# Six norms of a two-model forward pass in float32: token tiles, row halves, and who makes the low halves of x

## The chip, the core and the metric

One core of a Trainium2 chip. The metric is the device time of one execution in microseconds (us): the median of the runs.

## The reference

Two blocks of a sequence model run one behind the other on x of 256 tokens by 1024 channels. The first block is a gated convolution and a three-pattern dilated attention, merged; the second has two layers, each an attention (12 heads over the tokens, 4 over 256 memory tokens) and a convolutional feed-forward part (FFN, 2 x 2816 wide). Between the parts stand norms over the channels, two rms norms (y = x · rsqrt(mean(x²) + eps) · g) and four layer norms:

```python
def layer_norm(x, g, b):
    xf = x.astype(jnp.float32)
    mu = xf.mean(-1, keepdims=True)
    var = jnp.square(xf - mu).mean(-1, keepdims=True)
    return ((xf - mu) * lax.rsqrt(var + LN_EPS) * g + b).astype(x.dtype)
...
        x = layer_norm(ALPHA * x + mix, ln1_g[layer], ln1_b[layer])
        ffn = conv_ffn(x, ffn_w_in[layer], ffn_conv_w[layer], ffn_conv_b[layer], ffn_w_out[layer])
        x = layer_norm(ALPHA * x + ffn, ln2_g[layer], ln2_b[layer])
```

## The kernel before

**Split products.** Every large matmul is float32 made of three: each operand is a high half (rounded to the matmul type) and a low half (the rest), and high·high, high·low and low·high are summed in PSUM. The weights come from HBM as one stream of blocks of 128 x 1024 through a ring of three buffers. For each block SyncE loads `raw`, ScalarE copies it to the high half `wh` (L417), VectorE subtracts to the low half `wl` (L815), and TensorE uses both. A block's load waits until the low half of the block three before it is made (`split_l`); its high half waits until TensorE has used that block (`used`).

**Order of work.** Each engine has a list of instructions written out by hand, with semaphores between them. `refill(i, b)` stands in ScalarE's and in VectorE's list and makes the half of block b + 3.

**The row blocks.** The output product of a part (`row`, L1378 to L1380) adds one block to `ysum`, four PSUM banks: two token tiles of 128 (t) by two column halves (n), 12 matmuls of 512 columns. In the last block the first token tile signals `half`, the second `used`.

**A norm.** Six of them, n0 to n5; n0 and n1 are rms norms, the others layer norms. By token tile: VectorE adds the residual to `ysum` and sums (L861), ScalarE squares with a running sum (L431), GpSimd makes 1/sqrt (L297, L299), VectorE scales z (L889, or L893 without mean; L934 in n0). TensorE transposes z in eight 128 x 128 pieces a tile into four PSUM banks (`turn_x`, L1398), between which it multiplies memory keys or values, which don't need x. Then x is made, transposed, channel tile by channel tile (k = 0 to 7): VectorE multiplies by gain and adds shift into `xf` (L833, L836; ScalarE for k = 6, 7, L450), ScalarE makes the high half `xh` (L442), and the low half `xl` = xf - xh is made by VectorE for even k (L825) and by GpSimd for odd k (L322). TensorE takes all three products of one k before the next (`two_stationary`, L1342 to L1344, 48 matmuls of 256 columns; in n3 the value blocks at L1759; in n0 `row`). Behind its low halves GpSimd makes the next residual, x in token layout: z times gain, and plus shift in n2 to n4, two or four instructions of 128 x 1024 (`tail`, L312 and L315).

**Around n2 and n4** an FFN follows: TensorE opens the `ysum` banks with zero matmuls (L1483), ScalarE and VectorE make the first product of the FFN (L712, L1239, L1242, L718, L1250, L722, L825), and the loop goes on with `stationary` (L1330 to L1332, 24 matmuls of 256 columns) and `row`.

```python
            def tail(nm, shift):
                pool.wait_ge(gb_in, 16 + 32 * (norms.index(nm) - 1))
                for t in range(NT):
                    norm_wait(pool, nm, "z", t + 1)
                    last = pool.tensor_tensor(x_tok[:, t, :], z[:, t, :], gb[:, 0, :], ALU.mult)
                    if shift:
                        chain.link(last)
                        last = pool.tensor_tensor(x_tok[:, t, :], x_tok[:, t, :], gb[:, 1, :], ALU.add)
                    last.then_inc(S[nm, "x"], 1)
```

## Time and profile before

| what | us |
|---|---|
| median of 3 runs | 1001.85 (1001.05 to 1003.83) |
| the profiled execution | 1001.48 |
| its span, first to last instruction | 999.7 |
| TensorE busy | 948.9 |
| VectorE busy | 664.5 |
| ScalarE busy | 527.0 |
| GpSimd busy | 127.9 |

The span is the profiled part of one execution, 1.8 us shorter than its own time. In the trace's rows PE is TensorE, DVE VectorE, ACT ScalarE, POOL GpSimd. The start and the length of an instruction are given; where two rows of one engine overlap, the second starts while the first drains, so the distance of two starts is the cost of one in a row of many. The length of a row holds time in which the instruction stood started but could not go on.

### The profile page before, as it was taken

To read this page: it belongs to the slowest core of one execution; us is meant where nothing else is said; L and a number is where in the kernel's file an instruction comes from. 1 tells how busy PE (TensorE), PEld (TensorE's weight loads), DVE (VectorE), ACT (ScalarE), POOL (GpSimd) and SP (SyncE) were. 2 spreads that over 40 slices of the span, in tenths; PEclk is the share of its full clock that TensorE was granted. 3 is DMA by queue.
4 is the path that set the end of the run, shared out by engine and by line. 5 is a ranking of instruction groups with operands and counts; after the bars stand their busy time and mean duration, and the time that the engine had idled before them with its cause. 6 is when DMAs were issued, how large, how long until landed. Compare 5 with 4: busy or idle time off the path is not lost.

```text
span 999.7 us, 19995 instructions
## 1 busy us (share of the span) xinstructions
PE 948.9 (95%) x7006; PEld 859.3 (86%) x7006; DVE 664.5 (66%) x1212; ACT 527.0 (53%) x967; POOL 127.9 (13%) x154
## 2 busy tenths in 40 slices
PE   8999999999999888999799999998899989999995
PEld 5899999999899877757699999987788679999995
DVE  5566666666666857965866666678567666666666
ACT  5545555555444648754555555545565455555553
POOL 3000000000100402630600000006100150000001
PEclk9999999999999999999999999999999999999998
DMA  7555555556465375314265555553754346555552
GB/s 256 181 190 178 178 178 182 178 175 226 148 210 188 125 254 158 120 37 148 86 231 190 187 188 189 189 193 108 243 179 152 105 148 205 188 184 189 184 189 77
DMA packets 48226, 172.89 MB, mean 173 GB/s; under 512 B 6031, under 2 KB 6479, under 8 KB 48060
## 3 DMA queue, kind: packets, MB, share of 16 engines
q1 hardware_dynamic: 44732, 159.78, 47.9%
q0 software_dynamic: 3456, 12.61, 4.1%
q8 instruction: 24, 0.39, 0.2%
q14 instruction: 14, 0.11, 0.0%
HBM read 171.29 MB, written 1.07 MB: 172 GB/s over the span
## 4 chain that ended last, share of the span: by engine, by line
PE 77%; DVE 10%; ACT 6%; DMA 4%; issue 2%; POOL 1%; SPq 0%; POOLq 0%; ACTq 0%; DVEq 0%
PE bank L1330 17%; PE bank L1331 17%; PE bank L1332 17%; PE ysum L1378 6%; PE ysum L1380 6%; PE ysum L1379 6%; DVE sb_wl L815 5%; DMA sb_raw<-in_stream 4%; ACT sb_wh L417 2%; PE bank L1409 1%; PE ysum L1416 1%; PE ysum L1423 1%; ACT sb_xh L442 1%; DVE sb_z L861 1%; ACT sb_pr L462 1%
## 5 line engine op out<-in xcount | busy, mean ns | idle before, releaser
L815 DVE TENSOR_TENSOR sb_wl<-sb_raw,sb_wh 128x1024 fp32r<-128x1024 f32 x300 | 388.4, 1297 | 169.2 <-ACT sb_wh L417 168.3
L1330 PE MATMUL bank<-sb_xh,sb_wh 128*128 128x256 f32 x1360 | 383.3, 282 | 3.2 <-DVE sb_t_a L1242 2.5
L1331 PE MATMUL bank<-sb_xl,sb_wh 128*128 128x256 f32 x1360 | 379.8, 279 | 0.0
L1332 PE MATMUL bank<-sb_xh,sb_wl 128*128 128x256 f32 x1360 | 379.8, 279 | 0.0
L417 ACT ACTIVATE sb_wh<-sb_raw 128x1024 fp32r<-128x1024 f32 x300 | 315.0, 1055 | 116.2 <-PE ysum L1380 46.7
L1330 PEld LDWEIGHTS bank<-sb_xh,sb_wh 128*128 128x128 f32 x1360 | 256.3, 188 | 12.6 <-DVE sb_t_a L1242 3.5
L1332 PEld LDWEIGHTS bank<-sb_xh,sb_wl 128*128 128x128 f32 x1360 | 257.9, 190 | 0.0
L1331 PEld LDWEIGHTS bank<-sb_xl,sb_wh 128*128 128x128 f32 x1360 | 255.4, 188 | 1.5
L1378 PE MATMUL ysum<-sb_wh,sb_mh 128*128 128x512 f32 x208 | 81.7, 393 | 3.6 <-DVE sb_ml L825 3.6
L1379 PE MATMUL ysum<-sb_wl,sb_mh 128*128 128x512 f32 x208 | 81.7, 393 | 0.0
L1380 PE MATMUL ysum<-sb_wh,sb_ml 128*128 128x512 f32 x208 | 81.6, 393 | 0.0
L297 POOL TENSOR_SCALAR sb_st<-sb_st 128x1 f32<-128x1 f32 x12 | 4.3, 358 | 492.6 <-ACT sb_pr L431 488.5
L722 ACT ACTIVATE sb_mh<-sb_t_c 128x256 fp32r<-128x256 f32 x44 | 18.4, 419 | 90.4 <-DVE sb_t_c L1250 90.4
L712 ACT ACTIVATE sb_t_a<-bank,sb_convf 128x256 f32<-128x256 f32 x44 | 24.9, 566 | 47.3 <-PE bank L1332 43.0
L1378 PEld LDWEIGHTS ysum<-sb_wh,sb_mh 128*128 128x128 f32 x208 | 39.5, 190 | 10.4 <-issue 3.9
L462 ACT ACTIVATE sb_pr<-sb_sc,sb_mx 128x128 f32<-128x128 f32 x80 | 35.6, 448 | 23.1 <-DVE sb_mx L909 23.1
L1380 PEld LDWEIGHTS ysum<-sb_wh,sb_ml 128*128 128x128 f32 x208 | 39.5, 190 | 8.3
L1379 PEld LDWEIGHTS ysum<-sb_wl,sb_mh 128*128 128x128 f32 x208 | 39.3, 189 | 6.4
L1239 DVE SCALAR_TENSOR_TENSOR sb_t_a<-bank,sb_convf,sb_t_a 128x255 f32<-128x255 f32 x44 | 21.2, 482 | 27.0 <-ACT sb_t_a L712 26.9
L1330 PE MATMUL bank<-sb_mixh,sb_wh 128*128 128x256 f32 x128 | 36.3, 283 | 0.8 <-DVE sb_wl L815 0.8
L825 DVE TENSOR_TENSOR sb_ml<-sb_t_c,sb_mh 128x256 fp32r<-128x256 f32 x44 | 21.2, 481 | 23.9 <-ACT sb_mh L722 23.9
L1331 PE MATMUL bank<-sb_mixl,sb_wh 128*128 128x256 f32 x128 | 36.0, 281 | 0.0
(265 smaller groups left out, 1439.0 us busy)
## 6 DMA issues: line engine op xcount, KB each, us to landing
sb_raw<-in_stream SPq DMA_DIRECT2D x300, 512.0 KB, 3.3
sb_bias<-rel_rows POOLq DMA_DIRECT2D x12, 384.0 KB, 3.8
sb_bias<-in_alibi POOLq DMA_DIRECT2D x8, 256.0 KB, 3.1
sb_gb<-in_ln_g POOLq DMA_DIRECT2D x4, 512.0 KB, 4.1
sb_gb<-in_ln_b POOLq DMA_DIRECT2D x4, 512.0 KB, 6.5
sb_x_tok<-in_x SPq DMA_DIRECT2D x2, 512.0 KB, 3.9
sb_memf<-in_mem_t POOLq DMA_DIRECT2D x1, 1024.0 KB, 6.2
out<-sb_x_tok SPq DMA_DIRECT2D x2, 512.0 KB, 2.6
```

Of the source, the lines that this page charges most:

```text
L417: act.activation(wh[slot][:, :, :], raw[slot][:, :, :], ACT.Copy).then_inc(split_h, 1)
L462: act.activation(to[:, branch, h, cols], src, ACT.Exp, bias=mx[:, c:c + 1], scale=-1.0, accum_out=den[:, c:c + 1]).then_inc(S[ph, "exp"], 1)
L712: act.activation(t_a[:, :], bank[0][:, 0:T], ACT.Identity, bias=convf[:, layer, bass.ds(i, 1), 3], scale=convf[:, layer, bass.ds(i, 1), 2] ...
L815: dve.tensor_tensor(wl[slot][:, :, :], raw[slot][:, :, :], wh[slot][:, :, :].bitcast(F32), ALU.subtract).then_inc(split_l, 1)
L825: dve.tensor_tensor(dst, src, high, ALU.subtract).then_inc(s, 1)
L1239: cf.link(dve.scalar_tensor_tensor(out=t_a[:, 1:T], in0=bank[0][:, 0:T - 1], scalar=convf[:, layer, bass.ds(i, 1), 1], in1=t_a[:, 1:T], op ...
L1330: pe.matmul(out, wh[slot][:, k, :], mov_h(k), start=k == 0, stop=False)
L1331: pe.matmul(out, wh[slot][:, k, :], mov_l(k), start=False, stop=False)
L1332: last = pe.matmul(out, wl[slot][:, k, :], mov_h(k), start=False, stop=k == KT - 1)
L1378: pe.matmul(out, th[:, t * P:(t + 1) * P], hw, start=start, stop=False)
L1379: pe.matmul(out, th[:, t * P:(t + 1) * P], lw, start=False, stop=False)
L1380: last = pe.matmul(out, tl[:, t * P:(t + 1) * P], hw, start=False, stop=stop)
```

## The change

1. **The last two row blocks by token tile** (`last_rows`): tile 0 of both blocks, then tile 1 of both. `half` comes after 12 of the 24 matmuls and not after 18; the second block's operand is needed after 6 and not after 12. VectorE's low half for one later block, which stood ahead of the sums, stands behind them (`soon`).
2. **Rows of z in halves**: VectorE scales 512 columns at a time and TensorE transposes each half when it is there.
3. **High halves from PSUM**: ScalarE makes all eight `xh` straight from the transposed z, with gain and shift, not from `xf`. VectorE still fetches k = 0 to 5 into `xf`, ScalarE 6 and 7, behind the high halves. VectorE fetches a bank only when ScalarE is through with it (k = 4, 5 the other way round, except in n0 and n3).
4. **Low halves**: VectorE makes seven (all but k = 1), GpSimd k = 1 alone. GpSimd's `tail` stands right behind that one.
5. **Low x last**: `two_stationary` takes the products with `xh` of all eight k, then those with `xl`; the value blocks of n3 and the row blocks of n0 do the same inside one block (`x_rows`). The memory products between the transposes are cut in other places (`memory_keys`; in n3 the first value block of the memory needs no norm and stands ahead of the transposes, in bank 3).
6. In n4 ScalarE makes the high half of block `B_FFN1 + 2` ahead of x.

```diff
+FETCHED = {nm: (0, 1, 2, 3, 4, 5) if nm in ("n0", "n3") else (4, 5, 0, 1, 2, 3)
+           for nm in ("n0", "n1", "n2", "n3", "n4")}
+LOW_DVE, LOW_POOL = (0, 2, 3, 4, 5, 6, 7), (1,)
...
             def low_odd(nm):
-                for k in range(1, KT, 2):
+                for k in LOW_POOL:
+                    norm_wait(pool, nm, "xf", FETCHED[nm].index(k) + 1)
             def norm_high(nm, g, b):
-                def high(k):
-                    if k < 6:
-                        norm_wait(act, nm, "xf", k + 1)
-                    else:
-                        norm_wait(act, nm, "xf_act", k - 5)
-                    act.activation(xh[:, k, :], xf[:, k, :], ACT.Copy).then_inc(S[nm, "xh"], 1)
-                for k in range(4):
-                    high(k)
-                norm_wait(act, nm, "turned", KT)
+                shift = [0.0 if b is None else gbt[:, b, k:k + 1] for k in range(KT)]
+                for k in range(KT):
+                    norm_wait(act, nm, "turned", k // 2 * 2 + 2)
+                    if k in (4, 5) and nm not in ("n0", "n3"):
+                        norm_wait(act, nm, "xf", 2)
+                    act.activation(xh[:, k, :], turned_x(nm, k), ACT.Identity, scale=gbt[:, g, k:k + 1],
+                                   bias=shift[k]).then_inc(S[nm, "xh"], 1)
                 for k in (6, 7):
-                    if k == 7:
-                        high(4)
-                    act.activation(xf[:, k, :], turned_x(nm, k), ACT.Identity,
-                                   scale=gbt[:, g, k:k + 1], bias=0.0 if b is None else gbt[:, b, k:k + 1]
-                                   ).then_inc(S[nm, "xf_act"], 1)
-                for k in range(5, KT):
-                    high(k)
+                    act.activation(xf[:, k, :], turned_x(nm, k), ACT.Identity, scale=gbt[:, g, k:k + 1],
+                                   bias=shift[k]).then_inc(S[nm, "xf_act"], 1)
             def exps(ph, branch, h, causal=True, to=pr):
...
                 def fetch(k):
-                    norm_wait(dve, nm, "turned", k // 2 * 2 + 2)
+                    if nm in ("n0", "n3") or k < 4:
+                        norm_wait(dve, nm, "xh", k // 2 * 2 + 2)
+                    else:
+                        norm_wait(dve, nm, "turned", k // 2 * 2 + 2)
...
-                def low_even(k):
+                def low_of(k):
+                    if k < 6:
+                        norm_wait(dve, nm, "xf", FETCHED[nm].index(k) + 1)
+                    else:
+                        norm_wait(dve, nm, "xf_act", k - 5)
...
-                for k in range(0, 6, 2):
-                    fetch(k)
-                    fetch(k + 1)
-                    low_even(k)
-                    if k == 0 and between is not None:
-                        between()
-                low_even(6)
+                if nm in ("n0", "n3"):
+                    for k in FETCHED[nm]:
+                        fetch(k)
+                        if k in LOW_DVE:
+                            low_of(k)
+                        if k == 0 and between is not None:
+                            between()
+                else:
+                    for k in FETCHED[nm][:4]:
+                        fetch(k)
+                    low_of(0)
+                    for k in FETCHED[nm][4:]:
+                        fetch(k)
+                    for k in LOW_DVE[1:5]:
+                        low_of(k)
+                for k in (6, 7):
+                    low_of(k)
+            def norm_sum(nm, last_block, alpha, centred, x_from, fill=(), soon=None):
...
+                if soon is not None:
+                    refill(0, soon)
...
-                    if centred:
-                        norm_wait(dve, nm, "mean", t + 1)
-                        dve.tensor_scalar(z[:, t, :], z[:, t, :], st[:, 4 + t:5 + t],
-                                          st[:, 10 + t:11 + t], ALU.add, ALU.mult).then_inc(S[nm, "z"], 1)
-                    else:
-                        norm_wait(dve, nm, "sum", t + 1)
-                        dve.tensor_scalar(z[:, t, :], z[:, t, :], st[:, 10 + t:11 + t], None,
-                                          ALU.mult).then_inc(S[nm, "z"], 1)
+                    norm_wait(dve, nm, "mean" if centred else "sum", t + 1)
+                    for n in range(2):
+                        part = z[:, t, n * 512:(n + 1) * 512]
+                        if centred:
+                            dve.tensor_scalar(part, part, st[:, 4 + t:5 + t], st[:, 10 + t:11 + t],
+                                              ALU.add, ALU.mult).then_inc(S[nm, "z"], 1)
+                        else:
+                            dve.tensor_scalar(part, part, st[:, 10 + t:11 + t], None,
+                                              ALU.mult).then_inc(S[nm, "z"], 1)
...
+                if k1 == KT:
+                    last.then_inc(used, 1)
             def two_stationary(b, nm):
                 ready(b + 2)
+                for k in range(KT):
+                    norm_wait(pe, nm, "xh", k + 1)
+                    for n in range(2):
+                        out, s = bank[n][:, 0:T], slot_of(b + n)
+                        pe.matmul(out, wh[s][:, k, :], xh[:, k, :], start=k == 0, stop=False)
+                        pe.matmul(out, wl[s][:, k, :], xh[:, k, :], start=False, stop=False)
                 for k in range(KT):
                     x_ready(nm)(k)
                     for n in range(2):
-                        out, s = bank[n][:, 0:T], slot_of(b + n)
-                        pe.matmul(out, wh[s][:, k, :], xh[:, k, :], start=k == 0, stop=False)
-                        pe.matmul(out, wh[s][:, k, :], xl[:, k, :], start=False, stop=False)
-                        last = pe.matmul(out, wl[s][:, k, :], xh[:, k, :], start=False, stop=k == KT - 1)
+                        last = pe.matmul(bank[n][:, 0:T], wh[slot_of(b + n)][:, k, :], xl[:, k, :],
+                                         start=False, stop=k == KT - 1)
                         if k == KT - 1:
                             last.then_inc(used, 1)
-            def wide(slot, part, bk, sh, sl):
...
-                    norm_wait(pe, nm, "xl_pool" if k % 2 else "xl_dve", k // 2 + 1)
+                    norm_wait(pe, nm, "xh", k + 1)
+                    if k in LOW_POOL:
+                        norm_wait(pe, nm, "xl_pool", LOW_POOL.index(k) + 1)
+                    else:
+                        norm_wait(pe, nm, "xl_dve", LOW_DVE.index(k) + 1)
                 return wait
...
+                    last.then_inc(used, 1)
+            def x_rows(nm, slot, parts, out, n_first=False):
+                def part(w, j, n):
+                    j = n if n_first else j
+                    return w[slot][:, 4 * j:4 * j + 4, :].rearrange("p k c -> p (k c)")
+                for k, j, t, n in parts:
+                    norm_wait(pe, nm, "xh", k + 1)
+                    tok = slice(t * P, (t + 1) * P)
+                    pe.matmul(out(t, n)[:, :], xh[:, k, tok], part(wh, j, n), start=k == 0, stop=False)
+                    pe.matmul(out(t, n)[:, :], xh[:, k, tok], part(wl, j, n), start=False, stop=False)
+                for k, j, t, n in parts:
+                    x_ready(nm)(k)
+                    last = pe.matmul(out(t, n)[:, :], xl[:, k, t * P:(t + 1) * P], part(wh, j, n),
+                                     start=False, stop=k == KT - 1)
                 last.then_inc(used, 1)
...
+            def last_rows(b, first, second, half, second_made=()):
+                ready(b + 1)
+                row_tile(slot_of(b), *first, 0, False, False)
+                ready(b + 2)
+                for made in second_made:
+                    pe.wait_ge(*made)
+                row_tile(slot_of(b + 1), *second, 0, False, True).then_inc(half, 1)
+                row_tile(slot_of(b), *first, 1, False, False).then_inc(used, 1)
+                row_tile(slot_of(b + 1), *second, 1, False, True).then_inc(used, 1)
...
                 ready(k + 1)
-                x_ready("n0")(k)
-                row(slot_of(k), xh[:, k, :], xl[:, k, :], k == 0, k == KT - 1)
+                x_rows("n0", slot_of(k), [(k, 0, t, n) for t in range(NT) for n in range(2)],
+                       lambda t, n: bank[4 + 2 * t + n], n_first=True)
...
             def memory_keys(b, nm):
-                for n in range(2):
+                def keys(n, k0=0, k1=KT):
                     ready(b + n + 1)
-                    stationary(slot_of(b + n), bank[2 + n][:, 0:T], lambda k: memh[:, k, :], lambda k: meml[:, k, :])
-                    turn_x(nm, n)
+                    stationary(slot_of(b + n), bank[2 + n][:, 0:T], lambda k: memh[:, k, :], lambda k: meml[:, k, :],
+                               k0, k1)
+                keys(0)
+                turn_x(nm, 0)
+                keys(1, 0, KT // 2)
+                turn_x(nm, 1)
+                keys(1, KT // 2, KT)
...
             ffn("f0", B_FFN0, "n2")
+            ready(B_VM + 1)
+            wide(slot_of(B_VM), 0, bank[3], memh, meml)
+            ready(B_VM + 2)
             norm_wait(pe, "n3", "mean", 1)
-            for n in range(2):
-                ready(B_VM + n + 1)
-                wide(slot_of(B_VM + n), n, bank[4], memh, meml)
-                turn_x("n3", n)
+            for t in range(NT):
+                turn_x("n3", t)
+                wide(slot_of(B_VM + 1), 1, bank[3], memh, meml, (t,))
```

The places in the order of instructions. VectorE at n2, from the sum of token tile 1 to the first low half of the FFN's product. Before (`sb_xl<-sb_pt,sb_xh` is a low half of x, `sb_pt<-ysum` a fetch into xf, `sb_wl` a weight block's low half):

```order
L861 SCALAR_TENSOR_TENSOR sb_z,sb_st<-sb_x_tok,ysum1 128x1024 [waits used]
L866 TENSOR_SCALAR sb_st<-sb_st 128x1 [waits dve_chain]
L889 TENSOR_SCALAR sb_z<-sb_z,sb_st 128x1024 [waits norm_mean,norm_rstd] x2
...
L836 TENSOR_SCALAR sb_pt<-ysum0,sb_gbt 128x256 [waits norm_turned] x2
L825 TENSOR_TENSOR sb_xl<-sb_pt,sb_xh 128x256 [waits norm_xh]
L836 TENSOR_SCALAR sb_pt<-ysum0,sb_gbt 128x256 [waits norm_turned] x2
L825 TENSOR_TENSOR sb_xl<-sb_pt,sb_xh 128x256 [waits norm_xh]
L836 TENSOR_SCALAR sb_pt<-ysum1,sb_gbt 128x256 [waits norm_turned] x2
L825 TENSOR_TENSOR sb_xl<-sb_pt,sb_xh 128x256 [waits norm_xh] x2
L815 TENSOR_TENSOR sb_wl2<-sb_raw2,sb_wh2 128x1024 [waits split_h]
```

and now:

```order
L881 TENSOR_SCALAR sb_st<-sb_st 128x1 [waits dve_chain]
L813 TENSOR_TENSOR sb_wl2<-sb_raw2,sb_wh2 128x1024 [waits split_h]
L908 TENSOR_SCALAR sb_z<-sb_z,sb_st 128x512 [waits norm_mean,norm_rstd]
...
L837 TENSOR_SCALAR sb_pt<-ysum1,sb_gbt 128x256 [waits norm_turned] x2
L837 TENSOR_SCALAR sb_pt<-ysum0,sb_gbt 128x256 [waits norm_xh] x2
L823 TENSOR_TENSOR sb_xl<-sb_pt,sb_xh 128x256 [waits norm_xh,norm_xf]
L837 TENSOR_SCALAR sb_pt<-ysum0,sb_gbt 128x256 [waits norm_xh] x2
L823 TENSOR_TENSOR sb_xl<-sb_pt,sb_xh 128x256 [waits norm_xh,norm_xf] x4
L823 TENSOR_TENSOR sb_xl<-sb_pt,sb_xh 128x256 [waits norm_xh,norm_xf_act] x2
L813 TENSOR_TENSOR sb_wl2<-sb_raw2,sb_wh2 128x1024 [waits split_h]
```

The low halves of x went from four to seven, six of them in one row behind the last fetch, and a weight block's low half moved between the sums and z. GpSimd at the same place, before:

```order
L322 TENSOR_TENSOR sb_xl<-sb_pt,sb_xh 128x256 [waits norm_xh] x4
L312 TENSOR_TENSOR sb_x_tok<-sb_z,sb_gb 128x1024 [waits norm_z,gb_in]
L315 TENSOR_TENSOR sb_x_tok<-sb_x_tok,sb_gb 128x1024 [waits pool_chain]
L312 TENSOR_TENSOR sb_x_tok<-sb_z,sb_gb 128x1024 [waits norm_z]
L315 TENSOR_TENSOR sb_x_tok<-sb_x_tok,sb_gb 128x1024 [waits pool_chain]
```

and now:

```order
L328 TENSOR_TENSOR sb_xl<-sb_pt,sb_xh 128x256 [waits norm_xh,norm_xf]
L317 TENSOR_TENSOR sb_x_tok<-sb_z,sb_gb 128x1024 [waits norm_z,gb_in]
L320 TENSOR_TENSOR sb_x_tok<-sb_x_tok,sb_gb 128x1024 [waits pool_chain]
L317 TENSOR_TENSOR sb_x_tok<-sb_z,sb_gb 128x1024 [waits norm_z]
L320 TENSOR_TENSOR sb_x_tok<-sb_x_tok,sb_gb 128x1024 [waits pool_chain]
```

The four instructions of the tail (two in n1) stand three low halves nearer to the start of x. TensorE's 48 matmuls of x in n2 began, for each k, with this, before:

```order
L1342 MATMUL bank0<-sb_xh,sb_wh0 128x256 [waits norm_xl_dve,split_l]
L1343 MATMUL bank0<-sb_xl,sb_wh0 128x256
L1344 MATMUL bank0<-sb_xh,sb_wl0 128x256
L1342 MATMUL bank1<-sb_xh,sb_wh1 128x256
L1343 MATMUL bank1<-sb_xl,sb_wh1 128x256
L1344 MATMUL bank1<-sb_xh,sb_wl1 128x256
```

and now begin with four matmuls for each k that wait for the high half alone:

```order
L1361 MATMUL bank0<-sb_xh,sb_wh0 128x256 [waits norm_xh,split_l]
L1362 MATMUL bank0<-sb_xh,sb_wl0 128x256
L1361 MATMUL bank1<-sb_xh,sb_wh1 128x256
L1362 MATMUL bank1<-sb_xh,sb_wl1 128x256
L1361 MATMUL bank0<-sb_xh,sb_wh0 128x256 [waits norm_xh]
```

The 16 matmuls with `xl` follow behind all of these.

## Rows read from the trace of the kernel before

**Rows 1.** The page, part 1: busy us (share of the span) and instructions.
```profile
PE 948.9 (95%) x7006; PEld 859.3 (86%) x7006; DVE 664.5 (66%) x1212; ACT 527.0 (53%) x967; POOL 127.9 (13%) x154
```

**Rows 2.** What TensorE waited for, whole span: total us, times, longest us.
```profile
PE ysum L1378 <- DVE sb_ml L825: 3.6, 2, 2.0
PE bank L1330 <- DVE sb_t_a L1242: 2.5, 2, 2.0
```

**Rows 3.** Timeline, norm n2: start us, us, engine, instruction, count, idle before and releaser.
```profile
467.67 0.42 DVE L825 TENSOR_TENSOR sb_mixl<-bank,sb_mixh 128x256 fp32r<-128x256 f32 x1
469.21 0.39 PE L1378 MATMUL ysum<-sb_wh,sb_mixh 128*128 128x512 f32 x1
471.95 0.28 PE L1330 MATMUL bank<-sb_memh,sb_wh 128*128 128x256 f32 x1
475.30 0.81 DVE L889 TENSOR_SCALAR sb_z<-sb_z,sb_st 128x1024 f32<-128x1024 f32 x1 [0.92 <-POOL sb_st L299]
476.18 1.09 PE L1398 MATMUL ysum<-sb_ident,sb_z 128*128 128x128 f32 x8 [1.31 <-DVE sb_z L889]
477.57 2.35 DVE L815 TENSOR_TENSOR sb_wl<-sb_raw,sb_wh 128x1024 fp32r<-128x1024 f32 x2
481.38 0.42 DVE L825 TENSOR_TENSOR sb_xl<-sb_pt,sb_xh 128x256 fp32r<-128x256 f32 x1
481.95 0.36 PE L1342 MATMUL bank<-sb_xh,sb_wh 128*128 128x256 f32 x1 [0.98 <-DVE sb_xl L825]
483.08 0.55 ACT L450 ACTIVATE sb_pt<-ysum,sb_gbt 128x256 f32<-128x256 f32 x1
483.10 0.99 DVE L836 TENSOR_SCALAR sb_pt<-ysum,sb_gbt 128x256 f32<-128x256 f32 x2
487.88 1.04 PE L1483 MATMUL ysum<-sb_zeros 128*128 128x512 bf16 x4
```

**Rows 4.** Timeline, just behind n2: GpSimd and VectorE, and what TensorE waited for.
```profile
486.52 2.39 POOL L312 TENSOR_TENSOR sb_x_tok<-sb_z,sb_gb 128x1024 f32<-128x1024 f32 x1
486.99 2.99 DVE L815 TENSOR_TENSOR sb_wl<-sb_raw,sb_wh 128x1024 fp32r<-128x1024 f32 x1 [1.03 <-ACT sb_wh L417]
488.98 3.23 POOL L315 TENSOR_TENSOR sb_x_tok<-sb_x_tok,sb_gb 128x1024 f32<-128x1024 f32 x1
...
490.95 0.38 PE L1330 MATMUL bank<-sb_xh,sb_wh 128*128 128x256 f32 x1 [2.03 <-DVE sb_t_a L1242]
492.17 3.34 POOL L312 TENSOR_TENSOR sb_x_tok<-sb_z,sb_gb 128x1024 f32<-128x1024 f32 x1
494.11 1.68 DVE L825 TENSOR_TENSOR sb_ml<-sb_t_c,sb_mh 128x256 fp32r<-128x256 f32 x1 [0.49 <-ACT sb_mh L722]
495.59 2.43 POOL L315 TENSOR_TENSOR sb_x_tok<-sb_x_tok,sb_gb 128x1024 f32<-128x1024 f32 x1
495.94 0.52 PE L1378 MATMUL ysum<-sb_wh,sb_mh 128*128 128x512 f32 x1 [2.00 <-DVE sb_ml L825]
```

**Rows 5.** Timeline, VectorE and TensorE behind norm n3.
```profile
688.40 14.19 DVE L815 TENSOR_TENSOR sb_wl<-sb_raw,sb_wh 128x1024 fp32r<-128x1024 f32 x5 [0.98 <-ACT sb_wh L417]
691.50 0.50 PE L1759 MATMUL ysum<-sb_wh,sb_xh 128*128 128x512 f32 x1 [2.32 <-DVE sb_wl L815]
```

**Rows 6.** Busy time by engine, granted clock (PEclk) of two stretches, at n2 and n4.
```profile
496.40:499.40 3.00, 3.00 (x9) 2.32 (x8) 3.00 (x2) 0.00 (x0) 2.70 (x3) 0.50 0.00 0
796.70:803.30 6.60, 6.06 (x29) 5.69 (x28) 5.35 (x11) 4.87 (x11) 3.62 (x5) 0.50 0.01 2
```

**Rows 7.** Timeline: last product before n1; TensorE behind n1, behind n4, in n0.
```profile
323.27 0.43 DVE L1042 SCALAR_TENSOR_TENSOR sb_ml<-sb_t_c,sb_mh 128x256 fp32r<-128x256 f32 x1 [0.54 <-ACT sb_mh L541]
344.64 0.35 PE L1358 MATMUL bank<-sb_wh,sb_xh 128*128 128x256 f32 x1 [2.06 <-DVE sb_wl L815]
806.18 1.04 PE L1483 MATMUL ysum<-sb_zeros 128*128 128x512 bf16 x4
18.40 0.50 PE L1378 MATMUL ysum<-sb_wh,sb_xh 128*128 128x512 f32 x1 [0.94 <-DVE sb_wl L815]
```

More of the change, by code:

```diff
@@ L1326, in _, with stationary @@
         def _(pe):
-            def stationary(slot, out, mov_h, mov_l):
-                for k in range(KT):
+            def stationary(slot, out, mov_h, mov_l, k0=0, k1=KT):
+                for k in range(k0, k1):
                     pe.matmul(out, wh[slot][:, k, :], mov_h(k), start=k == 0, stop=False)
@@ L1365, in wait @@
                 def wait(k):
-                    norm_wait(pe, nm, "xl_pool" if k % 2 else "xl_dve", k // 2 + 1)
-                return wait
-            def row(slot, th, tl, start, stop, half=None, bank7_read=None):
-                for t in range(NT):
-                    for n in range(2):
-                        out = bank[4 + 2 * t + n][:, :]
-                        if bank7_read is not None and t == n == 1:
-                            pe.wait_ge(*bank7_read)
-                        hw = wh[slot][:, 4 * n:4 * n + 4, :].rearrange("p k c -> p (k c)")
-                        lw = wl[slot][:, 4 * n:4 * n + 4, :].rearrange("p k c -> p (k c)")
-                        pe.matmul(out, th[:, t * P:(t + 1) * P], hw, start=start, stop=False)
-                        pe.matmul(out, th[:, t * P:(t + 1) * P], lw, start=False, stop=False)
-                        last = pe.matmul(out, tl[:, t * P:(t + 1) * P], hw, start=False, stop=stop)
-                    if t == 0 and half is not None:
-                        last.then_inc(half, 1)
-                last.then_inc(used, 1)
+                    norm_wait(pe, nm, "xh", k + 1)
@@ new lines, in wait, with row_tile @@
+                    if k in LOW_POOL:
+                        norm_wait(pe, nm, "xl_pool", LOW_POOL.index(k) + 1)
+                    else:
+                        norm_wait(pe, nm, "xl_dve", LOW_DVE.index(k) + 1)
+                return wait
+            def row_tile(slot, th, tl, t, start, stop, bank7_read=None):
+                for n in range(2):
+                    out = bank[4 + 2 * t + n][:, :]
+                    if bank7_read is not None and t == n == 1:
+                        pe.wait_ge(*bank7_read)
+                    hw = wh[slot][:, 4 * n:4 * n + 4, :].rearrange("p k c -> p (k c)")
+                    lw = wl[slot][:, 4 * n:4 * n + 4, :].rearrange("p k c -> p (k c)")
+                    pe.matmul(out, th[:, t * P:(t + 1) * P], hw, start=start, stop=False)
+                    pe.matmul(out, th[:, t * P:(t + 1) * P], lw, start=False, stop=False)
+                    last = pe.matmul(out, tl[:, t * P:(t + 1) * P], hw, start=False, stop=stop)
+                return last
@@ L1706, in finish @@
                 memory_out(ph, 1)
-                rows(6)
-                pe.wait_ge(S[ph, "ol"], 2)
-                rows(7)
+                last_rows(r0 + 6, (oh[:, 6, :], ol[:, 6, :]), (oh[:, 7, :], ol[:, 7, :]), half, ((S[ph, "ol"], 2),))
             pe.wait_ge(S["p3", "fill"], 3)
@@ L1751, in _ @@
                 ready(b + 1)
[L1752 to L1762 removed]
+                x_rows("n3", slot_of(b), [(2 * n + j, j, t, 0) for j in range(2) for t in range(NT)],
+                       lambda t, n: bank[5 + t])
             for n in range(2):
```

77 lines of the change are left out of this document (31 added, 46 removed).

## The prediction

> **What bounds the kernel now.** The page's busy line comes first: TensorE works 948.9 of 999.7 us [rows 1]. So a change can win only in the 51 us in which TensorE stands, and lose only where it makes TensorE stand. The table of TensorE's waits says for whom: in the FFNs behind n2 and n4 it waits for the low half of the product (3.6 us in two waits) and for the convolution's last tap (2.5 us in two) [rows 2]. The timeline of n2 shows the norm's chain [rows 3]: the last row block starts at 469.21, the memory keys at 471.95 (12 matmuls of 512 columns in 2.74 us, 0.228 each), z is scaled from 475.30 for 0.81 us, the first transposes start at 476.18 after 1.31 us of standing, the first x matmul at 481.95 after 0.98, and the 48 x matmuls are through at 487.88, where the bank opening starts: 0.12 us each. They hardly wait: x, at 1.4 us for two channel tiles on VectorE, keeps up.
>
> The rows behind n2 show the thing I build on [rows 4]. GpSimd's tail has four instructions of 1024 columns. Its first starts at 486.52 and ends at 488.91, which is 2.39 us. VectorE's weight subtraction starts at 486.99 and needs 2.99 us, though two of the same took 2.35 together at 477.57 [rows 3]: it ends 1.07 us after GpSimd's instruction, so it stood until then. GpSimd's second begins at 488.98, takes 3.23 us and so waited for VectorE. A subtraction of 256 columns, 0.42 us elsewhere [rows 3], takes 1.68 us at 494.11 and ends at 495.79, 0.28 us after GpSimd's third (492.17 + 3.34 = 495.51). Behind n3 five weight subtractions take 14.19 us [rows 5]; at 1.17 each they would take 5.9. So a VectorE subtraction with both inputs in SBUF and a GpSimd instruction exclude each other, and with both queues full they take turns, one each. A turn of GpSimd costs 2.2 us (2.39 and 2.43 undisturbed, less the start). Fetches from PSUM are not stopped.
>
> The Trainium skill has a narrower rule in "Advanced Engine Details and Errata", VectorE Performance Modes: the port is shared, and GpSimd and the two-port modes of VectorE block each other. A subtraction of two tensors isn't in such a mode; by that rule none of the low halves would wait; what the time would be then stands with rival (e). The same skill's "SBUF — State Buffer", Who interferes with whom, counts an instruction with two SBUF inputs in as well, and the 1.68 us side with it.
>
> **The change, part by part.** Times are dates of the profiled execution (1001.48 us; the median of the three runs is 0.37 above it).
>
> *Last two row blocks.* The second block's low half is now wanted after 6 matmuls. At n2 it is there at 467.67 + 0.42 = 468.09 [rows 3], the 6 matmuls end at 469.21 - 1.37 = 467.84: TensorE stands 0.3 us. At n1 the operand ends at 323.70 [rows 7] and 6 matmuls earlier than needed before means 323.01: 0.75 us. I take 0.25 in n3, 0.3 in n4. In return tile 0's chain starts 2 us earlier; but a weight subtraction of 1.2 us stands between the sums and z, and tile 1's sum starts 0.3 later, so z starts at 475.3 as before. Only its first half, 0.42 instead of 0.81, brings the transposes from 476.18 to 475.8. Two more VectorE instructions a tile cost nothing there, since TensorE transposes the first half meanwhile. SyncE's load behind the moved weight subtraction starts 3 us later; its block is used in the FFN's loop, 20 us on, which covers it.
>
> *x at n2, with nobody in the way.* From 475.8: 16 transposes (1.8) and the 24 key matmuls (2.9) end at 480.5. ScalarE's high halves from PSUM cost 0.45 each (0.55 a row, less overlap) [rows 3], the first at 478.6, so the 32 matmuls with xh run without a gap to 484.3. VectorE: z until 477.5, two weight blocks to 479.8, six fetches of 0.46 and one low half to 482.9, six low halves of 0.34 to 485.0. The 16 matmuls with xl then end at 486.2, against 487.88: **1.7 us won.**
>
> *x at n2 with the tail.* GpSimd has one low half and starts its tail at 482.5, before VectorE's six low halves, where it stood 4 us later before. The first turn lasts to 484.7; then a low half (0.3), a turn (2.2), and so on: low halves 2, 3, 4 and 5 end at 485.0, 487.5, 490.0 and 492.5, numbers 6 and 7 at 493.2. The x matmuls end at 493.7: **5.8 us late.** In exchange GpSimd is through when the FFN starts. The waits of 2.03 and 2.00 us at 490.95 and 495.94 [rows 4] shrink to 0.5 and 0.5 (the chain itself is 0.56 + 2 x 0.48 us against 1.04 of bank opening): 3.0 back. n2 costs **+2.8**.
>
> *The others, same working.* n4: here nothing but zero matmuls stands between rows and transposes, so z's first half decides, at 793.9; x could start at 796.2 and, unblocked, be through at 801.9. VectorE's low halves 2 to 7 are due from 799.3, the tail starts at 799.0, and four turns put the last at 810.0: the x matmuls, at 806.18 through [rows 7], end at 810.4, +4.2; its waits of 1.6 and 0.5 [rows 2] (less n2's share) and 0.65 for weights behind give back 1.6: **+2.6**. n3: the first value block of the memory no longer waits for the sum (its 1.0 us goes, and x comes that much earlier), low halves alternate with fetches, and four turns fall between them as well; the third value block's weights, ready for 691.50 [rows 5], come behind the seventh low half at 694.1, at 695.3: +3.8, less 1.7, since the weight blocks then come faster than TensorE's 2.74: **+2.1**. n1 has two turns and starts 0.8 late (the 0.75 above): x ends at 344.2, the next weights at 345.0 against 344.64 [rows 7]: **+0.4**. n0 has no tail: its first matmul comes 1.2 us earlier, but VectorE reaches the third weight block 0.2 later than for 18.40 [rows 7], and TensorE waits for that: **+0.2**. n5: tile 0 earlier, tile 1, which ends the kernel, the same: 0 (between -0.4 and +0.3).
>
> *The clock.* Behind waits of 2 us in n2 and in n4 the granted clock was 0.50, that is 1.2 and not 2.4 GHz, for 3.0 and 6.6 us at least [rows 6]; a stretch of 3.4 us at it costs 1.7. No row shows what a stall of 6 to 8 us brings. Bounds: nothing new (n2 and n4 had theirs) and one more stretch in each of three norms, 5.1. I take 2.0, a stretch more in n3 and a little in n4, since their stalls are the long ones.
>
> Sum: 0.2 + 0.4 + 2.8 + 2.1 + 2.6 + 0 + 2.0 = **+10.1**: 1011.6 for the profiled execution, 1012.0 for the median.
>
> **Rivals.** (a) *VectorE's row of low halves keeps the port.* In n1, n2 and n4 six short ones stand in a row; if GpSimd's first gets in only where VectorE pauses, the gains stay. For it: none of my rows has two 256-column subtractions in a row beside the tail. Against it: behind n3 five subtractions stood in a row and GpSimd had its turn in between. n1 then gives -1.5 (the next weights meet the tail, at 343.1 for 344.64), n2 -1.7, n4 -4.3 (x done at 801.9: the highs run at full clock), n3 +2.1 as above, n0 +0.2: -5.2, so 996.7. It decides if the tail's start slips from 482.5 to beyond 485.0. (b) *Half hidden:* the first turn falls into the matmuls with xh, which TensorE has until 484.3, in n2, n3 and n4, and the clock doesn't fall: 10.1 less 3 x 2.2 and less 2.0 is +1.5: 1003. It decides if low half 2 comes before the turn and not behind it. (c) *The clock goes down and stays* in all four norms: 5 to 7 instead of 2, 1017. (d) *The change doesn't do what it says:* the early half buys nothing since z starts when it did; that is in my sum already, and a z at 474.3, where 1/sqrt would allow it, would shift everything by 1 us a norm: 1008. (e) *No blocking of subtractions at all.* Then the gains and the waits behind both fall in: n1 -3.3, n2 -1.7 - 3.0, n3 -3.4 - 1.7, n4 -4.3 - 1.6, n0 +0.2: 983. The 1.68 us for 0.42 [rows 4] speak against it, and nothing for it. It is what the skill's narrower rule would give.
>
> **How the numbers follow.** Forecast with its spread, (c) and (d): 0.76, of which (c) 0.08 and (d) 0.08. Rival (a) 0.13, (e) 0.01, (b) 0.10. The measurement can tell about 0.3%, 3 us, from no change. Faster is (a) and (e), 0.14, with 0.01 from (b)'s lower side, 0.15; the same is (b), 0.1; slower is the rest, 0.75. The range reaches from (b)'s lower side, 1001, to one clock stretch above (c), 1019; (a) and the tails are left out, 0.2 in all. The forecast's own range is 1006 to 1018.
>
> **What would show it.** Right: low halves 2 to 5 (now L823) at 0.42 to 2.5 us long in n1 to n4, mean near 1.2; TensorE's waits for `sb_xl` of 2 us and more, several a norm, 20 us in all and more; the waits for the tap and for `sb_ml` under 1 us each; the clock at 0.50 behind n3. The first transposes of n2 some 0.4 us earlier relative to the last row block. Wrong: low halves at 0.42 us throughout with the tail behind them (rival a), or x matmuls through earlier than before.

## The result and the profile after

| | before | changed |
|---|---|---|
| median, lowest, highest, us (5 runs each) | 1001.85, 1001.05, 1003.83 | 1010.25, 1009.00, 1014.62 |
| ratio to before | | 1.0087, 95% interval 1.0071 to 1.0103 |
| profiled execution, span, us | 1001.48, 999.7 | 1014.62, 1013.0 |

The change makes the kernel 8.4 us slower; 1012.0 was forecast, in a range of 1001 to 1019. The profiled execution of the changed kernel is the longest of its five, so it holds more than the median does; a second profile (below) tells how much.

The changed kernel, page part 1, what TensorE waited for in the whole span (total, times, longest), and VectorE's two groups of subtractions by line (busy us, mean ns, idle before):
```profile
PE 955.7 (94%) x6998; PEld 865.1 (85%) x7006; DVE 677.2 (67%) x1237; ACT 529.0 (52%) x967; POOL 107.8 (11%) x139
...
PE bank L1366 <- DVE sb_xl L823: 15.5, 10, 2.0
PE ysum L1396 <- DVE sb_wl L813: 10.3, 2, 7.8
...
L813 DVE TENSOR_TENSOR sb_wl<-sb_raw,sb_wh 128x1024 fp32r<-128x1024 f32 x300 | 370.1, 1236 | 166.3 <-ACT sb_wh L423 165.3
...
L823 DVE TENSOR_TENSOR sb_xl<-sb_pt,sb_xh 128x256 fp32r<-128x256 f32 x35 | 41.7, 1233 | 0.3
```
Of the 13.3 us more in the span [rows 1], TensorE is busy for 6.8 and stands for 6.5. The waits for `sb_ml` and for the convolution's tap [rows 2] are gone from the head of the table; in their place stand ten waits for the low half of x. A low half of 256 columns, 0.42 us elsewhere [rows 3], takes 1.23 on the average. The 300 weight subtractions have become shorter (1236 ns, 1297 before), since GpSimd now meets the low halves more than them.

Norm n2 in the changed kernel, timelines of VectorE, GpSimd and TensorE (start us, us):
```profile
485.88 0.42 DVE L823 TENSOR_TENSOR sb_xl<-sb_pt,sb_xh 128x256 fp32r<-128x256 f32 x1
486.21 1.00 DVE L837 TENSOR_SCALAR sb_pt<-ysum,sb_gbt 128x256 f32<-128x256 f32 x2
487.12 10.53 DVE L823 TENSOR_TENSOR sb_xl<-sb_pt,sb_xh 128x256 fp32r<-128x256 f32 x6
497.58 1.21 DVE L813 TENSOR_TENSOR sb_wl<-sb_raw,sb_wh 128x1024 fp32r<-128x1024 f32 x1
...
486.86 2.38 POOL L317 TENSOR_TENSOR sb_x_tok<-sb_z,sb_gb 128x1024 f32<-128x1024 f32 x1
489.32 2.41 POOL L320 TENSOR_TENSOR sb_x_tok<-sb_x_tok,sb_gb 128x1024 f32<-128x1024 f32 x1
491.69 2.52 POOL L317 TENSOR_TENSOR sb_x_tok<-sb_z,sb_gb 128x1024 f32<-128x1024 f32 x1
494.29 2.41 POOL L320 TENSOR_TENSOR sb_x_tok<-sb_x_tok,sb_gb 128x1024 f32<-128x1024 f32 x1
...
489.67 0.47 PE L1366 MATMUL bank<-sb_xl,sb_wh 128*128 128x256 f32 x2 [0.81 <-DVE sb_xl L823]
492.15 0.48 PE L1366 MATMUL bank<-sb_xl,sb_wh 128*128 128x256 f32 x2 [2.02 <-DVE sb_xl L823]
494.64 0.76 PE L1366 MATMUL bank<-sb_xl,sb_wh 128*128 128x256 f32 x2 [2.01 <-DVE sb_xl L823]
497.13 1.62 PE L1366 MATMUL bank<-sb_xl,sb_wh 128*128 128x256 f32 x6 [1.73 <-DVE sb_xl L823]
```
Six low halves that need 2.1 us alone are spread over 10.53. Each of the first four is let through when one instruction of the tail ends (489.24, 491.73, 494.21, 496.70), and TensorE's pairs of x matmuls follow, 2.49 us apart. GpSimd itself hardly loses: 2.38 to 2.52 us an instruction, as undisturbed.

Behind n3, VectorE and TensorE:
```profile
695.96 4.80 DVE L823 TENSOR_TENSOR sb_xl<-sb_pt,sb_xh 128x256 fp32r<-128x256 f32 x3
700.69 3.48 DVE L813 TENSOR_TENSOR sb_wl<-sb_raw,sb_wh 128x1024 fp32r<-128x1024 f32 x3
...
701.96 0.79 PE L1396 MATMUL ysum<-sb_wh,sb_xh 128*128 128x512 f32 x1 [7.78 <-DVE sb_wl L813]
```
The third value block's weights stand in VectorE's queue behind all low halves; TensorE stands 7.78 us where it stood 2.32 [rows 5].

### The profile page after: what moved, and what is told of

It reads as the page before. It is cut to its first block, busy times and chain, and to the rows that moved or that the text cites. A ratio compares the mean times of both kernels' runs of the same rounds, so it can differ in the third digit from the quotient of the medians.

```text
span 1013.0 us, 20115 instructions
## 1 busy us (share of the span) xinstructions
PE 955.7 (94%) x6998; PEld 865.1 (85%) x7006; DVE 677.2 (67%) x1237; ACT 529.0 (52%) x967; POOL 107.8 (11%) x139
## 4 chain that ended last, share of the span: by engine, by line
PE 77%; DVE 11%; ACT 4%; issue 3%; DMA 3%; POOL 1%; SPq 0%; POOLq 0%; DVEq 0%; ACTq 0%
PE bank L1348 17%; PE bank L1349 17%; PE bank L1350 17%; PE ysum L1422 6%; PE ysum L1424 6%; PE ysum L1423 6%; DVE sb_wl L813 3%; DMA sb_raw<-in_stream 3%; DVE sb_xl L823 3%; PE bank L1469 1%; ACT sb_wh L423 1%; PE ysum L1476 1%; PE ysum L1483 1%; PE ysum L1396 1%; PE ysum L1400 1%
## 5 line engine op out<-in xcount | busy, mean ns | idle before, releaser
L813 DVE TENSOR_TENSOR sb_wl<-sb_raw,sb_wh 128x1024 fp32r<-128x1024 f32 x300 | 370.1, 1236 | 166.3 <-ACT sb_wh L423 165.3
L460 ACT ACTIVATE sb_pr<-sb_sc,sb_mx 128x128 f32<-128x128 f32 x80 | 35.5, 445 | 23.4 <-DVE sb_mx L927 23.4
L823 DVE TENSOR_TENSOR sb_xl<-sb_pt,sb_xh 128x256 fp32r<-128x256 f32 x35 | 41.7, 1233 | 0.3
```

Source lines behind the costliest of these rows:

```text
L460: act.activation(to[:, branch, h, cols], src, ACT.Exp, bias=mx[:, c:c + 1], scale=-1.0, accum_out=den[:, c:c + 1]).then_inc(S[ph, "exp"], 1)
L813: dve.tensor_tensor(wl[slot][:, :, :], raw[slot][:, :, :], wh[slot][:, :, :].bitcast(F32), ALU.subtract).then_inc(split_l, 1)
L823: dve.tensor_tensor(dst, src, high, ALU.subtract).then_inc(s, 1)
```

## The experiments

Ratios are to the kernel before on the same chip, with their 95% intervals. Two chips were used, one for the first four experiments and one for the others; the kernel before has medians of 1004.5 to 1005.6 us on them, some 3 us more than in the first table.

### The tail later

```
 def tail(nm, shift):
     pool.wait_ge(gb_in, 16 + 32 * (norms.index(nm) - 1))
+    norm_wait(pool, nm, "xl_dve", len(LOW_DVE))
```


> The changed kernel, but GpSimd's tail (x_tok from z, gain and shift) waits in n1 to n4 until VectorE's seventh low half is done. If the turns of the port are the loss: the low halves behind the first take 0.34 to 0.45 us each (mean under 0.5 instead of 1.23), TensorE's waits for sb_xl fall from 15.5 us to under 1.5, the wait of 7.8 us in n3 shrinks to under 3, and in exchange waits of 1 to 2 us for the tap and for the low half of the product come back behind n2 and n4. Time 993 to 999 us. If something else makes the low halves slow (late high halves, the row of short instructions itself, the bank of PSUM): they stay at 1.2 us on the average and the time stays within 3 us of 1010.

Measured: 998.69 us, ratio 0.9942 (0.9924 to 0.9961). One wait turns the loss into a gain. VectorE's low halves and TensorE's largest waits:
```profile
L824 DVE TENSOR_TENSOR sb_xl<-sb_pt,sb_xh 128x256 fp32r<-128x256 f32 x35 | 13.6, 433 | 0.3
...
PE bank L1349 <- DVE sb_wl L814: 5.0, 7, 1.8
PE bank L1470 <- ACT sb_k_s L775: 3.7, 1, 3.7
PE ysum L1397 <- DVE sb_wl L814: 3.7, 3, 2.5
PE bank L1349 <- DVE sb_t_a L1261: 3.4, 2, 2.7
```
1233 ns fell to 433, no wait for `sb_xl` is left, and the waits for the tap are back (2.7 us behind n2). Nothing else was touched, so the place of the tail beside VectorE's low halves was the loss, not the seven low halves as work.

### The low halves divided as before

```
-LOW_DVE, LOW_POOL = (0, 2, 3, 4, 5, 6, 7), (1,)
+LOW_DVE, LOW_POOL = (0, 2, 4, 6), (1, 3, 5, 7)
```


> The changed kernel with the low halves divided as before (GpSimd 1, 3, 5, 7; VectorE 0, 2, 4, 6). If the turns are the loss: the tail starts only behind GpSimd's fourth low half, some 3 us later, VectorE has 2 or 3 low halves behind the fetches and they meet GpSimd's own short ones (0.7 to 0.85 us each), not the tail; x is through near 487 in n2's terms, about as early as before, and the time is 998 to 1003 us. If it is the high halves from PSUM, the value blocks with the low x last or the row blocks that cost the time, it stays at 1008 to 1012.

Measured: 999.63 us, ratio 0.9952 (0.9934 to 0.9971). The rest of the change, without this division, is worth 4.8 us. GpSimd makes four low halves again, so the tail also starts later: this run alone doesn't part the number of VectorE's low halves from the start of the tail, the run before does.

### This division alone, in the kernel before

```
-for k in range(1, KT, 2):      # GpSimd
+for k in (1,):
...
     low_even(k)                # VectorE
+    if k:
+        low_even(k + 1)
```


> The kernel before with one part of the change alone: VectorE takes seven low halves, GpSimd one, everything else as before. If the turns are the loss, this part alone makes the kernel slower: low halves of 2 to 2.5 us, TensorE's waits for sb_xl 10 to 20 us in all, 1010 to 1018 us. If the loss comes from the other parts, the time stays within 3 us of 1002, since VectorE only has 1.3 us more to do in each norm.

Measured: 1017.33 us, ratio 1.0127 (1.0100 to 1.0154): 12.8 us lost. With the 4.8 won by the rest this gives 8.0 us lost, beside 8.4 for the whole change in the first table and 6.5 by its ratio when it was run again (below). Each of these ratios is known to 2 or 3 us, and within that the parts add up. TensorE's waits and the low halves in it:
```profile
PE bank L1345 <- DVE sb_xl L825: 16.4, 13, 1.6
...
L825 DVE TENSOR_TENSOR sb_xl<-sb_pt,sb_xh 128x256 fp32r<-128x256 f32 x35 | 40.1, 1186 | 1.4 <-ACT sb_xh L442 0.6
```

### The tail at its place, in pieces of 256 columns

```
-last = pool.tensor_tensor(x_tok[:, t, :], z[:, t, :], gb[:, 0, :], ALU.mult)
+for q in range(4):
+    c = slice(q * T, (q + 1) * T)
+    last = pool.tensor_tensor(x_tok[:, t, c], z[:, t, c], gb[:, 0, c], ALU.mult)
...
```


> The changed kernel with the tail at its place, but in pieces of 256 columns (16 instructions in n2 to n4, 8 in n1, instead of 4 and 2). If VectorE and GpSimd take turns by instruction, a low half waits for one piece of 0.6 to 0.7 us instead of 2.4: low halves of 1.0 us instead of 2.4, x through 4 to 5 us earlier in n2 and n4, time 998 to 1004 us. If GpSimd keeps the port until its row of work is done, or if its whole time is what VectorE loses, cutting changes nothing: 1008 to 1013 us.

Measured: 997.8 us, ratio 0.9930 (0.9906 to 0.9953). TensorE and GpSimd in n2:
```profile
488.47 0.48 PE L1370 MATMUL bank<-sb_xl,sb_wh 128*128 128x256 f32 x2 [0.41 <-DVE sb_xl L827]
489.34 0.47 PE L1370 MATMUL bank<-sb_xl,sb_wh 128*128 128x256 f32 x2 [0.39 <-DVE sb_xl L827]
490.21 0.47 PE L1370 MATMUL bank<-sb_xl,sb_wh 128*128 128x256 f32 x2 [0.40 <-DVE sb_xl L827]
...
488.12 0.79 POOL L322 TENSOR_TENSOR sb_x_tok<-sb_x_tok,sb_gb 128x256 f32<-128x256 f32 x1
488.99 0.79 POOL L319 TENSOR_TENSOR sb_x_tok<-sb_z,sb_gb 128x256 f32<-128x256 f32 x1
489.86 0.79 POOL L322 TENSOR_TENSOR sb_x_tok<-sb_x_tok,sb_gb 128x256 f32<-128x256 f32 x1
```
One low half, one piece, 0.87 us apart instead of 2.49. So what a low half waits for is one instruction of GpSimd, not GpSimd's row of work: the turns are by instruction. The tail as work became dearer (0.73 us a piece undisturbed, 2.9 for four against 2.38), and the kernel still got faster.

### The low halves of n1 from PSUM

```
-low(xl[:, k, :], xf[:, k, :], xh[:, k, :].bitcast(F32), S[nm, "xl_dve"])
+dve.scalar_tensor_tensor(out=xl[:, k, :], in0=turned_x(nm, k), scalar=gbt[:, g, k:k + 1],
+                         in1=xh[:, k, :].bitcast(F32), op0=ALU.mult, op1=ALU.subtract
+                         ).then_inc(S[nm, "xl_dve"], 1)          # n1, k < 6
```


> The changed kernel, but in n1 VectorE makes low halves 0, 2, 3, 4 and 5 from the transposed rows in PSUM (gain times PSUM, less the high half) instead of from the fetched copy in SBUF; nothing else moves. If only an instruction with two SBUF inputs is held up by GpSimd: these take 0.43 to 0.5 us each beside the tail in n1 and TensorE's wait of 2.01 us for sb_xl there is gone or under 0.5, while n2 to n4 keep waits of 2 us; time 1 to 2 us less than the changed kernel. If every VectorE instruction is held up: the two of 2.4 us stay in n1.

Measured: 1010.93 us, ratio 1.0065 (1.0040 to 1.0090), the same as the changed kernel on this chip (next run), so the forecast of 1 to 2 us less isn't borne out by the time. The timeline of n1 is plain all the same, VectorE and GpSimd:
```profile
339.19 1.65 DVE L848 SCALAR_TENSOR_TENSOR sb_xl<-ysum,sb_gbt,sb_xh 128x256 fp32r<-128x256 f32 x4
340.76 3.31 DVE L823 TENSOR_TENSOR sb_xl<-sb_pt,sb_xh 128x256 fp32r<-128x256 f32 x2
...
338.88 4.92 POOL L317 TENSOR_TENSOR sb_x_tok<-sb_z,sb_gb 128x1024 f32<-128x1024 f32 x2
```
Four low halves with one input in PSUM take 0.41 us each in the middle of GpSimd's 1024 columns; the two behind them, with both inputs in SBUF, take 3.31 and are through at 344.07, just behind the end of its second instruction (343.80). TensorE's wait moved to those two (1.41 us). The edit changed the instruction's kind along with its input. The kernel before settles which of the two counts, in the FFN behind n2, between rows that were shown [rows 4]:
```profile
493.22 0.41 DVE L1250 TENSOR_TENSOR sb_t_c<-bank,sb_t_b 128x256 f32<-128x256 f32 x1
```
This is a TENSOR_TENSOR like the low half, with one input in PSUM. It takes 0.41 us beside GpSimd's third instruction, which lasts until 495.51; the low half of the product at 494.11, both inputs in SBUF, takes 1.68 beside the same one. So the input counts, not the kind.

The Trainium skill's narrower rule ("Advanced Engine Details and Errata", VectorE Performance Modes) names only the two-port modes; taken alone, it would leave a plain subtraction unhindered, and these rows show it held up. Its "SBUF — State Buffer", Who interferes with whom, draws the line where these rows do, at two SBUF inputs.

### The changed kernel again

> The changed kernel once more, on the chip of these runs. Its first profile was 3.7 us late at the end of n0 already, against 0.8 in the variants of it. If that was the start of that one run (first weights 1.2 us later) and a stretch at the lower clock behind it: here n0's third weight block is waited for near 19 us and the rows behind are 0.8 to 1.3 us later than before; if it belongs to the change, 3 us and more again. Ratio to before 1.006 to 1.012.

Measured: 1010.98 us, ratio 1.0065 (1.0041 to 1.0089); profiled 1010.65, span 1009.0. n0 is 0.6 us later than before, not 3.7: the rest was that one execution. Both profiles against the one of before, how much each stretch adds to TensorE's lateness:

| stretch, by dates of before | forecast | first profile | second |
|---|---|---|---|
| n0 (to 273.86) | +0.2 | +3.7 | +0.6 |
| n1 (to 441.98) | +0.4 | +0.6 | +1.7 |
| n2 and its FFN (to 673.6) | +2.8 | +2.8 | +2.2 |
| n3 (to 721.38) | +2.1 | +2.8 | +2.0 |
| up to n4's last rows (790.5) | 0 | +1.1 | +0.5 |
| n4, its FFN, n5 | +2.6 | +2.3 | +2.3 |
| the clock, apart | +2.0 | in the above | in the above |
| sum | +10.1 | +13.3 | +9.3 |

The stretches end behind the last row blocks. So the stand in n3's last rows (0.41 us) is in the n2 row, and that in n4's (0.48) makes up a good part of the row "up to n4's last rows"; the forecast had 0.25 and 0.3 for them in the rows of n3 and n4.

### TensorE kept busy in its stands

```
 for k in range(KT):
+    if k in {"n1": (3,)}.get(nm, (3, 4, 5)):
+        ...
+        for _ in range(7):
+            pe.matmul(bank[3][:, :], zeros[:, 0:P], zeros[:, :], start=True, stop=True)
     x_ready(nm)(k)
```


> The changed kernel with seven zero matmuls (1.5 us of TensorE, into a bank nobody reads) ahead of the x matmuls of the channel tiles whose low half comes late: tile 3 in n1, tiles 3, 4 and 5 in n2 and n4. They lie inside the stands of 2.0 us, so the stands stay as long and only TensorE's idle time in them goes. If the clock that falls behind such stands is a cost of its own: no stretch at 0.50 behind n1, n2 and n4 (three of 3.4 us or more, 1.7 us each), and the time is 3 to 5 us less than the changed kernel: ratio to before 1.001 to 1.004. If the stands alone cost the time, or the clock falls all the same: ratio 1.006 to 1.010 as without them.

Measured: 1010.62 us, ratio 1.0061 (1.0041 to 1.0082). Busy time and granted clock (third value from the end) of the same stretches, n2, n4 and n0, here and, in the second fence, in the changed kernel run again:
```profile
486.00:505.00 19.00, 15.59 (x88) 10.59 (x88) 16.20 (x16) 8.03 (x12) 9.44 (x6) 1.00 0.43 136
810.00:825.00 15.00, 12.49 (x68) 8.38 (x67) 12.55 (x14) 5.96 (x8) 6.56 (x5) 1.00 0.48 152
20.00:24.00 4.00, 4.00 (x12) 3.13 (x11) 1.41 (x2) 0.16 (x1) 0.00 (x0) 0.57 0.87 250
```
```profile
486.00:505.00 19.00, 12.29 (x65) 9.55 (x64) 16.83 (x16) 8.14 (x14) 9.73 (x6) 0.82 0.40 131
810.00:825.00 15.00, 9.92 (x49) 7.64 (x50) 12.70 (x14) 5.68 (x8) 6.72 (x5) 0.77 0.46 143
20.00:24.00 4.00, 4.00 (x19) 3.26 (x19) 1.50 (x3) 1.06 (x1) 0.00 (x0) 1.00 0.92 263
```
The clock stayed at 2.4 GHz behind n1, n2 and n4, and the median hardly moved. The two traces say where the gain went. They are one execution of each. Over n2 and its FFN this kernel is 0.3 us shorter, over n4 and its FFN 0.4: TensorE's first FFN matmuls are faster, and then it waits for the tap and the low half of the product (0.69 and 0.43 us) where it waited 0.16, since VectorE's chain sets the pace there. Over n1 and the part behind it, it is 2.4 us shorter. Of these 0.9 are there by 398 us and belong to n1; the other 1.5 come at 398 to 443, where the other execution had a second stretch at 1.2 GHz, at 403 to 406.5, which these matmuls don't touch. In n0, where nothing was edited, the time from 20 to 23.4 us ran at 1.2 GHz here and at 2.4 there, with TensorE busy throughout, and it is 1.9 us later behind it (third block 0.17 later, the mixer 2.07). So the stretches of 6.8 us behind a stand cost 0.3 to 0.9 us, as TensorE would have waited there for a part of the time anyhow, and those of 3.4 us in the midst of its work 1.5 to 1.9, about half their length. The kernel's time tells only that the filled stands of three norms together are worth little: the medians are 0.4 us apart, and that difference is known to some 2 us.

### The last two row blocks alone, in the kernel before

The whole of that part: rows by token tile, z in halves, the keys between the transposes, the moved weight subtraction.

> The kernel before with only the last two row blocks by token tile, z in halves and the keys between the transposes; the low halves, the high halves and the x matmuls as before. By the prediction this buys 0.4 us in n2 (transposes earlier), costs 0.3 to 0.8 elsewhere and is hidden for the most part: ratio to before 0.997 to 1.001. If the loss of the change had a part here, the ratio would be above 1.002.

Measured: 1003.47 us, ratio 0.9976 (0.9957 to 0.9994): 2.4 us won, at the good end of what was expected. So it has no part in the loss.

### The tail late and in pieces

```
+norm_wait(pool, nm, "xl_dve", len(LOW_DVE))
+at = {"n2": B_FFN0 + 4, "n4": B_FFN1 + 4}.get(nm)
...
+        if at is not None:
+            pool.wait_ge(split_l, at + 8 * t + 2 * q)
```


> The changed kernel with the tail behind the seventh low half and in pieces of 256 columns; in n2 and n4 one piece goes to each weight block of the FFN behind. If turns by instruction are all that the tail costs: low halves under 0.5 us, no wait over 0.5 us for the tap or the low half of the product behind n2 and n4 (each had 0.6 to 2.7 us with the tail late and whole), and the time lies 2 to 6 us below the late tail: ratio to before 0.988 to 0.993. If the late tail's gain is used up by weights that come late, it stays at 0.994.

Measured: 991.92 us, ratio 0.9875 (0.9856 to 0.9895). Both gains come together: low halves of 435 ns, and no wait over 0.70 us for the tap or the product behind n2 and n4 (0.5 was expected, and a ratio of 0.988 at the best). What is left in n3 shows on VectorE:
```profile
697.45 0.69 DVE L1312 COPY sb_z<-ysum 128x512 f32<-128x512 f32 x1 [5.57 <-POOL sb_x_tok L328]
...
705.64 0.29 DVE L937 CUSTOM_DVE_ANT_0 sb_sc<-bank,sb_bias 128x128 f32<-128x128 f32 x1 [4.19 <-DMA sb_bias<-rel_rows]
```
The value copies write where z lies and wait for the tail; the bias that the scores need is loaded behind the tail and behind two loads of gains.

### Two more moves

```
+if k == 4 and between is not None:      # VectorE, n0: behind low half 4
+    make_low(2, 3)
...
-make_low(2, 3)                          # VectorE, behind n0's last low half
...
-load_gb(a[g][row], a[b][row])           # GpSimd
 if nm == "n3":
     pool.wait_ge(S["p3", "max"], 12 * PAIRS2)
     for i in range(PAIRS2):
         relative("p5", i, 4)
+load_gb(a[g][row], a[b][row])
```


> The kernel with the late tail in pieces, and two more moves: in n0 VectorE splits the third weight block behind low half 4 instead of behind the last, and in n3 GpSimd loads the next gains only behind the p5 bias loads. If the wait of 2.5 us at 18.7 in n0 is the weight block behind the row of low halves: it goes below 1.5 us and all that follows is 0.8 to 1.3 us earlier. If the loads of gains delay the weight stream in n3: the wait of 3.3 us for ScalarE's k_s near 700 goes below 1.5; if not, it stays. Ratio to before 0.984 to 0.988, that is at the best 3 us less than without the two moves.

Measured: 986.07 us, ratio 0.9821 (0.9802 to 0.9840), the best version here, 18 us below the kernel before, and better than the 0.984 that was expected at the best. VectorE at the first scores behind n3, and what TensorE waited for:
```profile
701.53 0.29 DVE L939 CUSTOM_DVE_ANT_0 sb_sc<-bank,sb_bias 128x128 f32<-128x128 f32 x1 [0.27 <-PE ysum L1480]
...
PE bank L1480 <- ACT sb_k_s L784: 3.5, 1, 3.5
...
PE ysum L1407 <- DVE sb_wl L823: 1.8, 2, 1.0
```
n0's wait of 2.5 us is 0.98, and the rows behind it are 0.75 us earlier. In n3 I had named the wrong wait: the one for `sb_k_s` stayed (3.5), since ScalarE too has a copy of values that waits for the tail (7.62 us); what went is VectorE's 4.19 us for the bias.

## Why the prediction was right, and where it was not

**The turns.** Right in mechanism and in dates. The dates of the forecast are those of the profile before, and ahead of n2's last two row blocks the profile after is 4.33 us behind it. The prediction put low halves 2 to 5 of n2 at 485.0, 487.5, 490.0 and 492.5; TensorE takes the late ones at 489.67, 492.15, 494.64 and 497.13, which less 4.33 is 485.3, 487.8, 490.3 and 492.8. The tail starts at 486.86, on that scale 482.5, as forecast. The x matmuls end at 494.4, forecast 493.7. n3's third value block: 701.96, less the 6.71 us of lateness ahead of n3's last rows, is 695.3, as forecast. One sign was set too high: the waits for `sb_xl` are 15.5 us in all and not 20, because n3's stand falls to the weights instead (7.8 us).

**Rival (a)**, that six low halves in a row keep the port, falls with the rows of n2: GpSimd gets its turn between any two of them. (b) falls too: the first turn covers low half 2, which TensorE waits for 0.81 us. The late tail and the one in pieces show that the price hangs on the tail's place and on the length of its pieces. (e) falls with the same rows. For (c) see the clock.

**What is given back.** Forecast 3.0 us in n2 and 1.6 in n4; measured more. In n2 the x matmuls end 6.5 us late against the start of the last two row blocks (5.8 forecast), and in the FFN's loop 2.4 are left of that, so that 4.1 came back. In n4, counted in the same way, x is 5.0 late (4.2), and 2.9 are left in the loop: 2.1 came back. I left 0.5 us in each of the two waits behind n2; neither is left.

**The last row blocks.** The stands there are longer than I had them: with what the restart costs they are 0.95, 0.49, 0.41, 0.48 and 0.41 us in n1 to n5, 2.7 in all, where I had 0.75, 0.3, 0.25, 0.3 and, for n5, none. (The rows that I took n1's from give 323.70 less 323.01, which is 0.7 and not 0.75.)

**A term that was too small: n0.** +0.2 forecast, +0.6 measured, with a wait of 2.5 us for the third weight block at 18.7 to 20.5 us in every profile of this order. I had the block 0.2 later than before; it is 0.6, in an execution whose first x matmul came 1.0 earlier (10.75 against 11.71): it stands in VectorE's list behind all of n0's low halves, and moving it ahead of the last ones took 1.5 us off the wait. And I gave no price to a lower clock there, which, where it comes, costs 1.6 to 1.9, since n0 is bound by TensorE. In the first profile it came (21.8 to 25.2 us), and the first weights were split 1.2 us later than in the profile of before. That profile has the third block 1.5 us later than the second one (20.52 against 19.03) and 1.6 more behind it, which with the 0.6 makes its 3.7.

**The clock.** I charged 2.0 us for it. Stretches at 1.2 GHz did come, behind n1 to n4, in the first profile for 6.8, 10.2, 10.2 and 6.8 us, where the kernel before had 3.4, 3.4, none and 6.8, and TensorE's busy time rose by 6.8 us. That is not their price: filling the stands of n1, n2 and n4 took theirs away and changed the time by less than it can tell. So what rival (c) supposed, the lower clock in all four norms, came true, and its time of 1017 did not. Of the 2.0 I can say neither that it was there nor that it wasn't; the stand in n3 was not filled, and its share stays open.

**Rival (d)**, z at 474.3, did not come: z starts at 479.44, which less 4.33 is 475.1, forecast 475.3. The first transposes of n2 start at 480.04, on that scale 475.7, forecast 475.8: 0.5 us earlier than before where 0.4 was forecast. (Against the keys they are 0.96 earlier, but the keys come 0.49 later themselves, by the stand in the last rows.) Alone, rows and halves win 2.4 us, and with the high halves from PSUM and the low x last 4.8.

So the sum, 10.1 against 9.3 and 13.3 in the two profiles, is right for the turns. In the rest part of the agreement is luck: without the 2.0 for the clock, which no run bears out, it is 8.1, and terms too small (n0, n1, the stands in the last rows) stand beside a give-back that was taken too small as well. By the median the change costs 8.4 us, and 6.1 when it was run again, so the forecast was somewhat high.

## What to carry to other kernels

Before moving two-input SBUF work from GpSimd to VectorE, ask what GpSimd will then start earlier, and whether VectorE's urgent short instructions stand behind it: each pays one whole GpSimd instruction. Work on GpSimd that nobody needs soon belongs behind the urgent row, in short pieces, each released by an event at which VectorE is about to wait for somebody else. A risen busy time of TensorE beside a low granted clock was a loss in full here only where TensorE didn't wait right behind it.
